# Delta rule of a fused layer kernel: the first level's two products are put side by side, and the values, the state's update and the remainders are moved behind them

## The reference, cut to what matters

```python
a_mat = lower + jnp.eye(C)                      # lower: strict lower triangle of (k*beta) k^T * decay
rhs = concatenate([v * beta, kb * exp(gc)])
sol = triangular_solve(a_mat, rhs, lower=True, unit_diagonal=True)
...
def step(S, xs):
    v_new = u_i - w_i @ S
    o_i = qd_i @ S + qk_i @ v_new
    S = S * gt_i + kd_i.T @ v_new
```

## Time and profile before

| | |
|---|---|
| median of three runs | 1688.0 us (1684.64 to 1688.14) |
| the profiled execution's own time | 1685.96 us |
| its span in the trace | 1684.0 us |
| TensorE busy | 1633.1 us (97%) |
| VectorE busy | 1073.2 us (64%) |
| ScalarE busy | 838.1 us (50%) |
| granted TensorE clock, mean | 0.996 |

### The profile page before, as it was taken

One profiled execution on the slowest core, in us unless ns is written; L12 is line 12 of the kernel. 1 busy time (PEld: TensorE's weight loads), 2 busy tenths in 40 slices (PEclk: granted clock), 3 DMA queues, 4 the chain that ended last, 5 costly groups with the idle time before them and its releaser, 6 DMA issues.

```text
span 1684.0 us, 24234 instructions
## 1 busy us (share of the span) xinstructions
PE 1633.1 (97%) x9896; PEld 1335.8 (79%) x9896; DVE 1073.2 (64%) x1626; ACT 838.1 (50%) x1223; POOL 56.4 (3%) x56
## 2 busy tenths in 40 slices
PE   6999998889999999999999999999999999999998
PEld 3878877775788888878878888888888878788886
DVE  3789567865655458547875545755466658865554
ACT  4444577554454445647454444544444645554542
POOL 0000133200000000000000000000000000000000
PEclk9999999999999999999999999999999999999999
DMA  9332420012565555534455555655555434555452
GB/s 366 152 143 107 154 98 28 28 52 97 192 265 181 177 198 200 200 125 175 165 208 179 190 184 193 249 176 189 184 200 200 176 135 165 197 186 192 175 194 105
DMA packets 39693, 285.52 MB, mean 170 GB/s; under 512 B 4384, under 2 KB 4512, under 8 KB 5920
## 3 DMA queue, kind: packets, MB, share of 16 engines
q1 hardware_dynamic: 37840, 270.71, 44.8%
q0 software_dynamic: 1744, 13.27, 2.0%
HBM read 282.91 MB, written 1.05 MB: 169 GB/s over the span
## 4 chain that ended last, share of the span: by engine, by line
PE 89%; DVE 5%; DMA 2%; issue 2%; ACT 2%; SPq 0%; DVEq 0%; ACTq 0%
PE psum L439 85%; PE psum L442 4%; DMA ring<-stream 1%; DVE cst L2075 1%; DVE cst L2069 1%; DVE cst L2313 1%; DMA arena<-stream 1%; DVE ring_lo L2075 1%; DVE arena L2069 1%; ACT w_hi L1594 0%; ACT arena L1594 0%; DVE arena L2562 0%; ACT cst L1594 0%; DVE arena L2567 0%; DVE sblk L2142 0%
## 5 line engine op out<-in xcount | busy, mean ns | idle before, releaser
L2075 DVE TENSOR_TENSOR ring_lo<-ring,w_hi 128x1024 fp32r<-128x1024 f32 x416 | 489.0, 1221 | 221.9 <-ACT w_hi L1594 221.2
L1594 ACT ACTIVATE w_hi<-ring 128x1024 fp32r<-128x1024 f32 x416 | 415.8, 1053 | 285.3 <-DMA ring<-stream 232.7
L439 PE MATMUL psum<-w_hi,xT_hi 128*128 128x512 f32 (+1 forms) x1184 | 452.0, 391 | 3.8 <-ACT w_hi L1594 1.9
L439 PE MATMUL psum<-w_hi,xT_lo 128*128 128x512 f32 (+1 forms) x1184 | 446.8, 387 | 0.2
L439 PE MATMUL psum<-ring_lo,xT_hi 128*128 128x512 f32 (+1 forms) x1184 | 446.8, 386 | 0.0
L439 PEld LDWEIGHTS psum<-w_hi,xT_hi 128*128 128x128 f32 x1184 | 221.9, 188 | 49.8 <-issue 5.4
L439 PEld LDWEIGHTS psum<-w_hi,xT_lo 128*128 128x128 f32 x1184 | 222.0, 188 | 46.4 <-DVE xT_lo L2075 0.9
L439 PEld LDWEIGHTS psum<-ring_lo,xT_hi 128*128 128x128 f32 x1184 | 222.6, 188 | 43.7
L2069 DVE TENSOR_TENSOR arena<-psum,arena 128x256 f32<-128x256 f32 (+2 forms) x148 | 73.6, 509 | 144.7 <-ACT arena L1907 121.5
L1594 ACT ACTIVATE arena<-psum 128x512 f32<-128x512 f32 (+5 forms) x157 | 82.6, 555 | 153.0 <-PE psum L439 118.2
L439 PE MATMUL psum<-w_hi,hfT_hi 128*128 128x512 f32 x352 | 137.7, 391 | 0.0
(11 more groups left out here) (252 smaller groups left out, 1818.8 us busy)
## 6 DMA issues: line engine op xcount, KB each, us to landing
ring<-stream SPq DMA_DIRECT2D x249, 1024.0 KB, 4.8
arena<-ln_params POOLq DMA_DIRECT2D x6, 1024.0 KB, 6.6
arena<-par POOLq DMA_DIRECT2D x2, 1730.0 KB, 10.0
arena<-stream SPq DMA_DIRECT2D x3, 1024.0 KB, 7.0
ring<-biases SPq DMA_DIRECT2D x2, 1024.0 KB, 4.9
cst<-const POOLq DMA_DIRECT2D x1, 1728.0 KB, 7.3
arena<-x_in SPq DMA_DIRECT2D x1, 1024.0 KB, 5.1
arena<-ctx_in SPq DMA_DIRECT2D x1, 1024.0 KB, 9.1
```

Source lines behind the costliest of these rows:

```text
L439: owe(nc.tensor.matmul(o, lhsT, rhs, start=first, stop=last), sem)
L1594: return A(o, i, ACT.Copy)
L2075: return V_.tensor_tensor(o, a, b, ALU.subtract)
```

## The change

The order of calls is changed on three engines; no instruction is added or removed. On TensorE the second product of the first level follows `key_products` directly, `values` comes behind it (for n = 2 only behind `second_level_out`), and `state_update` comes behind `last_level_in` (n = 1, 2) or behind `second_level_in` (n = 3). For n = 2, `key_products(3)` is split: the first direction stands ahead of `first_level_in(2)`. ScalarE's and VectorE's streams follow; on VectorE `lower` comes first, and `remainders` moves behind `first_level` for n = 2, and behind `state_outputs(2)` for n = 3.

```diff
-            def key_products(n):
-                for d in range(2):
+            def key_products(n, directions=(0, 1)):
+                for d in directions:
...
             for n in range(1, 4):
+                if n == 2:
+                    key_products(3, (0,))
                 first_level_in(n)
-                if n < 3:
-                    key_products(n + 1)
+                if n == 1:
+                    key_products(2)
+                elif n == 2:
+                    key_products(3, (1,))
                 else:
                     query_products(2, 0)
                     query_products(2, 1)
-                values(n - 1)
                 first_level_out(n)
-                state_update(n - 1)
+                if n != 2:
+                    values(n - 1)
                 second_level_in(n)
                 if n == 1:
                     decays(3, 0, 0)
                 elif n == 2:
                     attention_keys((0,))
+                else:
+                    state_update(2)
                 second_level_out(n)
+                if n == 2:
+                    values(1)
...
                 last_level_in(n)
+                if n < 3:
+                    state_update(n - 1)
...
@@ ScalarE
             for n in range(4):
                 first_level(n)
-                if n:
+                if n in (1, 2):
+                    second_level_in(n)
+                diagonal_to_64(n)
+                if n == 3:
+                    for d in range(2):
+                        evacuate(("VN", 2, d), Vn[d])
+                if n in (0, 3):
+                    second_level_in(n)
+                if n < 3:
+                    second_level_to_64(n)
+                if n == 0:
+                    act.wait_ge(S("zeros"), 2)
+                if n in (1, 2):
                     for d in range(2):
                         evacuate(("VN", n - 1, d), Vn[d])
-                diagonal_to_64(n)
+                diagonal(n, lambda d: (early32[d][1 - d], late32[d][1 - d]), "Xt_late")
+                if n == 3:
+                    state(2)
+                    second_level_to_64(n)
                 if n:
-                    state(n - 1)
-                second_level_in(n)
-                if n == 0:
-                    second_level_to_64(n)
-                    act.wait_ge(S("zeros"), 2)
-                diagonal(n, lambda d: (early32[d][1 - d], late32[d][1 - d]), "Xt_late")
-                if n:
-                    second_level_to_64(n)
...
                     copy(Yl[d][late[d], :], ps[late[d], :]).then_inc(free, 1)
+                if n in (1, 2):
+                    state(n - 1)
@@ VectorE
             for n in range(4):
+                if n < 3:
+                    lower(n + 1)
                 if n > 1:
                     state_values(n - 1)
-                    remainders(n - 1)
-                if n < 3:
-                    lower(n + 1)
-                else:
+                if n == 3:
                     state_outputs(2)
+                    remainders(2)
+                first_level(n)
+                if n == 2:
+                    remainders(1)
+                elif n == 3:
                     query_factors(2, 0)
-                first_level(n)
+                    query_factors(2, 1)
                 part(SPLIT_0)
...
-            query_factors(2, 1)
             state_values(3)
```

## The result

The changed kernel takes 1693.13 us (median of six runs, 1691.18 to 1695.62) against 1687.66 us before (six runs beside it, 1684.64 to 1688.88). The ratio is 1.0033, 95% interval 1.0023 to 1.0044: 5.5 us slower, where 0.9 us faster was forecast and the range ended at 1690.8 us. The profiled execution took 1691.18 us, 5.2 more than that of before.

A forecast was written before the change was run, and what follows sets the result against it. Prediction saw the turns bound by waits through TensorE's small products, VectorE's subtraction of `Z4` and the inversion to `X32`, with `values` in front. Turns of +0.7, +2.6 and -4.2 summed to -0.9 us: 1687.1 us, range 1681.6 to 1690.8.

The forecast's parts named there:

- Turn 1, +0.7 us: First products of chunk 2 come 0.7 us later, behind `key_products(3, (0,))`, which waits for ScalarE's first `kbT` copy.
- Turn 2, +2.6 us: First products of chunk 3 come at t+28.2 against t+25.6, by a line of ScalarE and TensorE work behind `Y5`.
- Turn 3, -4.2 us: Waits and a stop go, leaving TensorE's own work in line, 17.8 us against 21.98 us before.
- The stops: TensorE's stops go by instruction count: inside `values(0)`, mid `second_level_in` in turn 2, behind `values(2)`; each nothing to 1.9 us.
- a second stop in turn 2: Cache-line borders could add another TensorE stop in turn 2, making the sum -0.3 us instead of -0.9.
- Slower: the clock: Rival: TensorE's 2.7 us idle before `first_level_out` in turn 2 lowers the clock, costing 5.2 us; 1692.3 us, chance 0.09.
- The removal counts in full: Rival: all three `values` leave VectorE's path, nothing replacing them; -6.7 to -8.1 us, halved about -5.5; 1682.5 us, chance 0.23.
- ScalarE alone sets everything: Rival: only idle time moves; turns 1 and 2 worse, turn 3 better by 2.2 us; +1.1 us, 1689.1 us, chance 0.13.

The follow-up runs named there:

- e4: Kernel before with the new order in turns 1 and 3 only, `key_products(3)` whole behind `first_level_in(2)`; 1682.44 us, ratio 0.9969.
- e9: Changed kernel with `state_values(1)` ahead of `lower(3)`, `values(1)` right behind `first_level_out(2)` and `remainders(1)` ahead of `first_level(2)`; 1686.11 us, ratio 0.9986.
- e3: Kernel before with the new order in turn 3 alone; 1684.18 us, ratio 0.9981.
- e6: Changed kernel with `values(1)` right behind `first_level_out(2)` and `remainders(1)` ahead of `first_level(2)`; 1689.31 us, ratio 1.0008.
- e1: Changed kernel with three unused 128x512 products added ahead of `first_level_out(2)`; 1693.96 us, ratio 1.0041.
- e2: Changed kernel with `state_values(1)` ahead of `lower(3)` on VectorE; 1692.20 us, ratio 1.0024.
- e5: Changed kernel with three, one and two unused 128x512 products ahead of `first_level_out(2)`, `second_level_in(2)` and `second_level_out(2)`; 1692.38 us, ratio 1.0026.
- e8: Kernel before with the new order in turn 2 alone, with `key_products(3)` split; 1695.35 us, ratio 1.0047.
- e7: Kernel before with the new order in turns 1 and 3, turn 2 old, but with `key_products(3)` split; 1685.69 us, ratio 0.9985.
- e10: Changed kernel with `state_values(1)` ahead of `lower(3)`, `values(1)` behind `first_level_out(2)`, `remainders(1)` ahead of `first_level(2)`, `key_products(3)` unsplit; 1682.34 us, ratio 0.9969.
- e11: Kernel before with sixteen unused 32x32 products ahead of a transpose group of chunk 2; 1687.61 us in a single run.

## Why the prediction was wrong, step by step

**Turn 1, +0.7 us: right in its mechanism.** Measured +0.35. ScalarE idles 1.74 us before its copy of `Y5`, where about 2 was forecast; the subtraction of `Z4(1)` is at 280.37; the first products of chunk 2 at 301.63 stand directly behind the first half of `key_products(3)`, while `X32(2)` had been written at 300.03. e4 shows that without the split the turn would have been shorter than before.

**Turn 2, +2.6 us: the step that failed.** The sum took every product behind the wait for the bank at full clock, `values(1)` at 3.8 us above all, and had no stop in `second_level_out`. The turn took 34.49 us, not 28.2, and these 6.3 us are the whole miss. The ladder up to `Y5` held: `first_level_out` at t+5.14 (forecast 5.0), `Z4` full at t+6.4 (6.3), `remainders(1)` 1.25 us between the transposes and the shuffles (1.3), `Y5` done at t+9.31 (8.85). From there to chunk 3's first products I had 19.35 us and it was 25.2. Term by term: `values(1)` 7.1 instead of 3.8, +3.3; `second_level_out` 1.9 with its last piece instead of 1.2, and the `nakT` transposes, 1.1 us at the lower clock, outlasting the 0.8 allowed for ScalarE's copy, together about +1.0; a stop of 2.02 us in `second_level_out` that the sum had not, +2.0; the rest -0.5. So the clock accounts for some 4.3 us and the stop for 2.0. By products and place this is read from the trace. In e9 the fall of the clock in turn 2 is gone, and with it the loss, together with the wait of 2.76 us; its stops in turn 2 (1.26, 0.31 and 0.44 us) add up to 2.0 us instead of 2.8, so they are not gone but lie elsewhere.

**Turn 3, -4.2 us: right.** Measured -3.96, and -3.7 us as a kernel of its own (e3, whose turn 3 is 3.5 shorter in the profile).

**The stops.** I placed one stop in turn 2, from two rows with the same distance of five units, and took it as a period. The border that stopped TensorE for 2.02 us is the one behind it, one unit further on. The sentence on a second stop in turn 2 named this case and priced it at 0.6 us; the new order puts 126 short products between the two borders, into 5.4 us. In turn 1 the border inside `values(0)` cost nothing: the copy of `Y5` starts at 284.58 instead of 285.25, and the turn's only stop, 0.15 us, comes one unit later at 286.43, behind `Y5`. That explains the 0.35 us by which turn 1 is shorter than forecast.

**The rivals.** "Slower: the clock" was the right mechanism, with a chance of 0.09. That its time, 1692.3 us against 1693.1, came so near is partly luck: it priced the clock at 5.2 us, which cost some 4.3, and had nothing for the stop of 2.0. What misled me was the condition. I looked for one idle time between 2.02 and 3.53 us and asked on which side 2.76 lies. e6 shows that this wait is enough here, and e1 and e2 that it is not needed: behind it lie four more pieces of small products and waits, which I had summed for time and not looked at together. In the changed kernel TensorE is busy 3.76 us of 7.35 and then 4.20 of the next 7.02. The second figure alone tells nothing, since before has as thin a piece in its turn 2, at full clock:

```profile
314.76:321.76 7.00, 4.15 (x142) 3.39 (x141) 6.18 (x27) 6.73 (x17) 0.00 (x0) 1.00 0.01 2
```

"The removal counts in full" failed in turns 1 and 2 as described; "ScalarE alone sets everything" had turn 3 too small.

**What stays open.** What exactly lowers the clock: e5 was busy for 12.5 of 14.7 us before it fell, e9's short fall in turn 3 has neither thin place ahead of it, and before itself has a wait of 2.02 us without a fall. Each arrangement was profiled once. About 2 of the 3.5 us by which e4's gain and e8's loss do not add up. And what, beyond 1.1 to 1.3 us in turn 1, the 3 to 4 us between the kernels with and without the split are.

## What to carry to other kernels

When dense work is moved off a ladder of small products, what follows may no longer run at full clock: look at the waits and small products that are left in a row before costing it, and price both clock levels. In this kernel's profiles it took both, `values` back in the ladder and the wait removed, to keep turn 2 at full clock; filling the gaps with unused products did not do it reliably. A change made in three turns of a loop should be timed turn by turn; here two turns gained 5.5 us (e4), and the third lost more than that. A stop that recurs after a fixed number of instructions may be one of several borders, most of them without a stop; count the smallest unit and check where each falls in the new order.

## What the runs showed of the hardware

- The granted clock fell to 0.50 and stayed there for 17.1 us (changed kernel), 20.5 (e2, e6) and 23.9 (e8), but only 3.4 us in e7, e9 and e10. TensorE was busy for most of it (9.78 us of 10.05 in the changed kernel, 18.71 of 20.50 in e6, all 3.42 in e9), so the clock did not return as soon as there was work.
- It fell with no wait or stop over 1.2 us in the turn ahead (e2, the longest 1.15 us), behind a run of 32-wide products with short waits and stops.
- TensorE stopped for 0.15 to 2.3 us (2.27 in e1) with no semaphore to wait for. In the traces of before, the changed kernel and e11 these stops come behind a record of its own stream whose number is 193 more than a multiple of 256, about 125.4 products apart or several times that, and most such borders show no stop.
